# Inverse roots of three recurrent heads by small GpSimd operations, and two latent value products placed behind a head's turn

## The reference

```python
h_ml = mlstm_chunkwise(q_ml, k_ml, v_ml, gates[..., :ML_HEADS], gates[..., ML_HEADS:])
h_ml = rmsnorm(h_ml, ml_head_norm.reshape(ML_HEADS, ML_V))     # h * rsqrt(mean(h * h) + EPS), 4 heads of 128
h_ml = h_ml * jax.nn.sigmoid(o_ml)
...
h_mla = causal_block_attention(q, k, kv[..., MLA_NOPE:])       # 8 latent heads, 4 query blocks of 128
return jnp.concatenate([h_ml, h_mla], axis=-1) @ w_out
```

## Time and profile before

| | |
|---|---|
| median of 3 runs | 1511.03 us (1510.55 to 1511.44) |
| the profiled execution | 1513.8 us, of which the span is 1512.0 us |
| granted TensorE clock, mean | 0.998 |
| busy in the span | PE 99%, DVE 75%, ACT 50%, POOL 41% |
| chain that ended last | PE 87%, ACT 4%, DVE 4% |

### The profile page before, as it was taken

How to read it: one execution, slowest core, us unless ns; L and a number is a source line. 1 busy time by engine, 2 the same in 40 slices (tenths; PEclk the granted TensorE clock), 3 DMA queues, 4 the chain that set the end, 5 groups by cost and what they waited for, 6 DMA issues and landing times.

```text
span 1512.0 us, 20174 instructions
## 1 busy us (share of the span) xinstructions
PE 1491.3 (99%) x6978; PEld 1231.2 (81%) x6978; DVE 1128.0 (75%) x1872; ACT 751.4 (50%) x1255; POOL 626.8 (41%) x280
## 2 busy tenths in 40 slices
PE   9999999999999999999999999999999999999998
PEld 7888888878888887888888888787778888888887
DVE  5689999997865445776776768788755887777776
ACT  6554333455562345754544345464963745444434
POOL 3455444332334432144444445451534344444451
PEclk9999999999999999999999999999999999999999
DMA  5343233345443323333333123233643432333551
GB/s 212 98 124 99 95 94 95 92 157 157 157 157 98 98 83 112 104 93 97 112 98 109 52 85 97 84 98 93 186 140 105 142 117 90 109 122 114 142 136 56
DMA packets 77026, 170.40 MB, mean 113 GB/s; under 512 B 22660, under 2 KB 39172, under 8 KB 76680
## 3 DMA queue, kind: packets, MB, share of 16 engines
q1 hardware_dynamic: 75920, 165.64, 35.2%
q10 hardware_dynamic: 1016, 3.61, 0.7%
HBM read 154.54 MB, written 14.69 MB: 112 GB/s over the span
## 4 chain that ended last, share of the span: by engine, by line
PE 87%; ACT 4%; DVE 4%; issue 3%; POOL 1%; DMA 1%; SPq 0%; DVEq 0%; ACTq 0%; POOLq 0%
PE bank L795 86%; DMA w_raw<-in_stream 1%; POOL w_lo L655 1%; ACT w_hi L1604 1%; DVE x_sq L2359 0%; ACT l_probs L2129 0%; DVE bias L2441 0%; ACT l_probs L2135 0%; ACT dn_first L1898 0%; POOL res L764 0%; DMA dn_raw<-in_stream 0%; PE bank L1214 0%; DVE res_tok L3421 0%; PE bank L905 0%; ACT ml_square L2080 0%
## 5 line engine op out<-in xcount | busy, mean ns | idle before, releaser
L655 POOL TENSOR_TENSOR w_lo<-w_raw,w_hi 128x1024 fp32r<-128x1024 f32 x191 | 473.2, 2487 | 518.1 <-ACT w_hi L1604 510.4
L795 PE MATMUL bank<-a_hi,w_hi 128*128 128x512 f32 (+1 forms) x1120 | 444.8, 397 | 2.2 <-DVE a_lo L3284 1.8
L795 PE MATMUL bank<-a_hi,w_lo 128*128 128x512 f32 (+1 forms) x1120 | 431.4, 385 | 0.0
L795 PE MATMUL bank<-a_lo,w_hi 128*128 128x512 f32 (+1 forms) x1120 | 431.2, 385 | 0.0
L1604 ACT CAST w_hi<-w_raw 128x1024 fp32r<-128x1024 f32 x199 | 204.6, 1046 | 174.9 <-DMA w_raw<-in_stream 174.5
L795 PEld LDWEIGHTS bank<-a_hi,w_hi 128*128 128x128 f32 x1120 | 210.5, 188 | 49.0 <-issue 4.2
L795 PEld LDWEIGHTS bank<-a_lo,w_hi 128*128 128x128 f32 x1120 | 210.6, 188 | 45.2 <-issue 3.4
L795 PEld LDWEIGHTS bank<-a_hi,w_lo 128*128 128x128 f32 x1120 | 210.4, 188 | 42.6
L667 POOL TENSOR_TENSOR dn_rest<-dn_raw,dn_second 128x1024 fp32r<-128x1024 f32 x39 | 93.7, 2431 | 248.3 <-DVE dn_rest L2734 248.3
L795 PE MATMUL bank<-dn_rest,f_hi 128*128 128x512 f32 x364 | 141.7, 389 | 0.0
L1898 ACT CAST dn_first<-dn_raw 128x1024 fp32r<-128x1024 f32 x54 | 55.6, 1047 | 157.9 <-DVE dn_raw L2715 157.9
(11 more groups left out here) (428 smaller groups left out, 2763.5 us busy)
## 6 DMA issues: line engine op xcount, KB each, us to landing
w_raw<-in_stream SPq DMA_DIRECT2D x199, 512.0 KB, 3.5
dn_raw<-in_stream SPq DMA_DIRECT2D x56, 512.0 KB, 3.6
p_parts<-d_parts SPq DMA_DIRECT2D x8, 640.0 KB, 3.9
d_turned<-p_parts SPq DMA_DIRECT2D x32, 160.0 KB, 3.3
l_turned<-p_parts SPq DMA_DIRECT2D x32, 160.0 KB, 3.1
p_parts<-l_parts SPq DMA_DIRECT2D x8, 384.0 KB, 3.3
res<-in_xT ACTq DMA_DIRECT2D x1, 2048.0 KB, 9.1
p_parts<-l_parts SPq DMA_DIRECT2D x8, 256.0 KB, 2.4
```

Of the source, the lines that this page charges most:

```text
L655: nc.gpsimd.tensor_tensor(w_lo[:, j, :], w_raw[:, j, :], w_hi[:, j, :].bitcast(F32), ALU.subtract).then_inc(w_lo_done, 1)
L795: return nc.tensor.matmul(o, l, r, start=start, stop=stop)
```

## The change

For heads 0 to 2 the root leaves ACT and the inverse leaves DVE. DVE adds one operation at `st` 8: it reads the bits of `mcol[:, 2]` as an integer, times -0.5 plus a constant, which is a first guess of the inverse root. POOL refines it by ten operations on 128x4 values (`inverse_root`), each waiting for the one before on `root_step`; the tenth posts `ml_inv`, which DVE's scaling at `st` 9 waits for. Head 3 keeps ACT's root. In POOL's list the three refinements stand behind `remainder(CH["OM"])`, behind the first eight residual products, and behind the second eight.

The value products of latent heads 1 and 5 move: head 1 from step 13 to 14, head 5 from 29 to 28, in both cases between the turn of a recurrent head and `ml_values`. The cast and low part of latent head 1 move one step later; those of head 5 stay.

```diff
+VALUES_AT = {9: 0, 14: 1, 17: 2, 21: 3, 25: 4, 28: 5}
+SPLIT_AT = {10: 0, 15: 1, 18: 2, 22: 3, 26: 4, 30: 5}
...
+            def stepped(ins):
+                ins.then_inc(sems["root_step"], 1)
+                root_steps[0] += 1
+                pool.wait_ge(sems["root_step"], root_steps[0])
+
+            def inverse_root(h):
+                part, slope, x, y = (mcol[:, i, :] for i in range(4))
+                pool.wait_ge(sems["ml_var"], h + 1)
+                stepped(nc.gpsimd.tensor_tensor(part, y, y, ALU.mult))
+                stepped(nc.gpsimd.tensor_tensor(part, part, x, ALU.mult))
+                stepped(nc.gpsimd.tensor_scalar(slope, part, 0.375, -1.25, ALU.mult, ALU.add))
+                stepped(nc.gpsimd.tensor_tensor(part, part, slope, ALU.mult))
+                stepped(nc.gpsimd.tensor_scalar(part, part, 1.0, 1.875, ALU.mult, ALU.add))
+                stepped(nc.gpsimd.tensor_tensor(y, y, part, ALU.mult))
+                stepped(nc.gpsimd.tensor_tensor(part, y, y, ALU.mult))
+                stepped(nc.gpsimd.tensor_tensor(part, part, x, ALU.mult))
+                stepped(nc.gpsimd.tensor_scalar(part, part, -0.5, 1.5, ALU.mult, ALU.add))
+                nc.gpsimd.tensor_tensor(y, y, part, ALU.mult).then_inc(sems["ml_inv"], 1)
...
             remainder(CH["OM"], CH["OM"] % RING)
+            inverse_root(0)
             behind_diagonals(2)
...
             for unit in (17, 18):
                 second_residual(unit, residual_steps[unit])
+            inverse_root(1)
             behind_diagonals(3)
...
             for unit in (23, 24, 25, 26):
                 second_residual(unit, residual_steps[unit])
+            inverse_root(2)
             behind_diagonals(4)
...
-                turned = n == ML_START + ML_EVERY + turned_at(1)
+                turned = n in [ML_START + ML_EVERY * h + turned_at(h) for h in range(ML_HEADS - 1)]
...
-                if n % 4 == 1 and n >= 9:
-                    latent_values(n // 4 - 2)
+                if n in VALUES_AT:
+                    latent_values(VALUES_AT[n])
...
                 if st == 7:
                     act.wait_ge(sems["ml_out"], 4 * (h + 1))
+                    if h >= 1:
+                        act.wait_ge(sems["ml_inv"], h)
...
-                if st == 8:
+                if st == 8 and h == ML_HEADS - 1:
                     act.wait_ge(sems["ml_var"], h + 1)
                     A.activation(mcol[:, 3, :], mcol[:, 2, :], ACT.Sqrt).then_inc(sems["ml_root"], 1)
...
+                    if h < ML_HEADS - 1:
+                        chained(m)
+                        m = V.tensor_scalar(mcol[:, 3, :].bitcast(I32), mcol[:, 2, :].bitcast(I32), -0.5, ROOT_SEED,
+                                            ALU.mult, ALU.add)
+                    m.then_inc(sems["ml_var"], 1)
...
                 if st == 9:
-                    dve.wait_ge(sems["ml_root"], h + 1)
-                    V.reciprocal(mcol[:, 3, :], mcol[:, 3, :]).then_inc(sems["ml_inv"], 1)
+                    if h == ML_HEADS - 1:
+                        dve.wait_ge(sems["ml_root"], 1)
+                        V.reciprocal(mcol[:, 3, :], mcol[:, 3, :]).then_inc(sems["ml_inv"], 1)
                     dve.wait_ge(sems["ml_inv"], h + 1)
```

More of the change, by code:

```diff
@@ L205 @@
 squares_added ssq_added ssqg_added start_hi start_ready start_scaled stat_ready stat_root tap_done
-topk_step uq_out vm_rows wi_copied wi_turned x2_done x2_gained apart_hi apart_lo dn_sum dn_done dn_evac b_sum b_cast b_ready z_done z_root y_written half_done half_rooted half_sums part_sq part_ssq qk_tanh post_tree post_sq first_w first_x p_stored p_landed
+topk_step uq_out vm_rows wi_copied wi_turned x2_done x2_gained apart_hi apart_lo dn_sum dn_done dn_evac b_sum b_cast b_ready z_done z_root y_written half_done half_rooted half_sums part_sq part_ssq qk_tanh post_tree post_sq first_w first_x p_stored p_landed root_step
 """
@@ L222 @@
 GATES_AT = 1
+ROOT_SEED = float(0x5F3759DF)
 LATE_CASTS = 17
+VALUES_AT = {9: 0, 14: 1, 17: 2, 21: 3, 25: 4, 28: 5}
+SPLIT_AT = {10: 0, 15: 1, 18: 2, 22: 3, 26: 4, 30: 5}
 def turned_at(h):
@@ L705, in _ @@
             pool.wait_ge(sems["qk_rows_zeroed"], 2)
+            root_steps = [0]
+            def stepped(ins):
[15 more added lines that the diff above has]
+                nc.gpsimd.tensor_tensor(y, y, part, ALU.mult).then_inc(sems["ml_inv"], 1)
             for c in range(CH["OA"], CH["OM"]):
@@ L2148, in _ @@
             for n in range(4 * MLA_HEADS):
-                if n % 4 == 2 and n >= 10:
-                    latent_hi(n // 4 - 2)
+                if n in SPLIT_AT:
+                    latent_hi(SPLIT_AT[n])
                 latent_scaled(n)
@@ L3109, in ml_score_step @@
                     dve.wait_ge(sems["ml_den"], h + 1)
-                    V.scalar_tensor_tensor(out=mcol[:, 2, :], in0=mcol[:, 2, :], scalar=1.0 / ML_V,
-                                           in1=mcol[:, 1, :], op0=ALU.mult, op1=ALU.add).then_inc(sems["ml_var"], 1)
+                    m = V.scalar_tensor_tensor(out=mcol[:, 2, :], in0=mcol[:, 2, :], scalar=1.0 / ML_V,
+                                               in1=mcol[:, 1, :], op0=ALU.mult, op1=ALU.add)
+                    if h < ML_HEADS - 1:
[3 more added lines that the diff above has]
+                    m.then_inc(sems["ml_var"], 1)
             def ml_step(h, st):
@@ L3226, in _ @@
                     latent_turn(n - 1)
-                if n % 4 == 2 and n >= 10:
-                    latent_lo(n // 4 - 2)
+                if n in SPLIT_AT:
+                    latent_lo(SPLIT_AT[n])
                 ml_rest(n)
```

## The result

The changed kernel took 1516.03 us (median of 8 runs, 1514.06 to 1517.71); the kernel before beside it 1511.39 us (8 runs, 1510.55 to 1513.67). The ratio is 1.0027 with a 95% interval of 1.0018 to 1.0036, 2.7 to 5.4 us: slower. The forecast was 1510.5 us, and its range ended at 1514.0.

The account below looks back on a forecast made before the run. PE, busy 99%, bounds it; only its waits and slow clock can be won. 0.2 + 1.3 - 1.5 + 0.3 + 0.2 (last a guess for freer ACT) = 0.5 us off the median: 1510.5 us, range 1507.0 to 1514.0.

Parts of the forecast that it names:

- ACT's roots out: Heads 0 to 2: two table loads fewer per head, 7.7 us off ACT, so ACT bounds no `sT` any more.
- POOL's ten steps: Each refinement chain on POOL takes 2.6 us, 2.7 with the wait for `ml_var`.
- The ISA row: Rival, chance 0.12: MODIFY_POOL_CONFIG, inside head 0's chain, costs up to 3.3 us: 1513 to 1516; forecast took nothing.
- Head 0: At head 0 nothing waits for POOL's chain; latent head 1's products cover PE's 0.23 us for `hml`: gain 0.2 us.
- Head 1: Chain ends in time for DVE's scaling at head 1, PE's 1.31 us wait for `sT` goes: gain 1.3 us.
- Head 2: Third chain queues behind POOL's `rstd` products, `sT` comes as late as before: PE's 1.5 us lead is lost.
- The port: POOL's small chain operations beside DVE's diagonals can be held up: 0.3 us or so, put into the range.
- Latent head 5 moved: After head 2: covers 0.78 us for `hml`, later bares 1.0 us; gain 0 to 0.3, 1.6 to 1.8 if clock holds.
- The base of the sum: The 0.5 us gain was taken off the median, 2.8 us below the profiled execution's 1513.8 us.
- the clock's 1.6 us: After head 2's waits the granted clock was 0.54 for 3.4 us, costing 1.6 us.
- the 5.2 us to win: PE's four waits at heads 0 to 2, 3.6 us, with the slow clock 5.2 us: 0.34% of the kernel.

Follow-up runs that it names:

- e9: e5 with latent head 5's products back at step 29: 1510.48 us, ratio .9985 to the kernel before.
- e3: Kernel before with only the new places of latent heads 1 and 5, no root moved: 1513.67 us, ratio 1.0009 to the kernel before.
- e4: Changed kernel with latent head 1's products alone back at step 13: 1514.65 us, ratio 1.0018 to the kernel before.
- e8: e4 with one refinement left out of each POOL root, 6 steps for 10: 1512.59 us, ratio .9997 to the kernel before.
- e5: e4 with POOL's eight residual products of units 23 to 26 moved behind the last `ml_lo`: 1511.93 us, ratio .9997 to the kernel before.
- e12: Changed kernel with only POOL's eight residual products of units 23 to 26 moved behind the last `ml_lo`: 1514.23 us, ratio 1.0011 to the kernel before.
- e6: e4 with the third head's root given back to ACT and DVE: 1513.29 us, ratio 1.0003 to the kernel before.
- e2: Changed kernel with latent heads 1 and 5 put back where they stood, POOL's roots kept: 1514.40 us, ratio 1.0012 to the kernel before.

## Why the prediction was wrong, by its own steps

- *ACT's roots out*: right. Six table loads are gone between 1035 and 1130 us (7 before, 1 left), and where POOL's roots are in time (e9) `sT` comes earlier at heads 1 and 2.
- *POOL's ten steps*, 2.6 us: nearly right. Most took 0.20 us and 0.28 from start to start, two steps of a chain 0.30 to 0.33, and the chain 2.95 us at heads 0 and 2. At head 1 three took 0.33 to 0.62 and the chain 3.4 (1082.95 to 1086.36).
- *The ISA row*: nothing, as taken. Step 3 of head 0 began 0.30 us after step 2, which excludes the rival's 3.3 us. The first call's 6 us, of the Trainium skill ("GPSIMD Engine Reference", section "2.1 Instruction dispatch"), don't show here either. That the measured 1516.03 is the time which the prediction worked out for that rival, about 1516, is chance.
- *Head 0*, gain 0.2: **this step failed first**, by 2.1 us. I gave latent head 1's products to the 0.23 us that they would cover and left out what they covered where they stood. From DVE's scaling to `sT` it is 1067.35 - 1064.38 = 3.0 us of DVE's own queue, and PE got to the next score 1.8 us sooner than that. e3 shows 1.4 us by the order alone, and the changed kernel has 0.5 more with GpSimd's chain. That nothing waits for the chain here was wrong too: DVE's scaling at 1064.38 had waited 0.61 us for POOL. With the products back ahead of the turn (e4) neither shows.
- *Head 1*, gain 1.3: right in kind, 0.8 in size. A wait of 0.46 for `sT` stayed, because the chain was 0.7 us longer than my 2.7; with four steps fewer (e8) it is gone.
- *Head 2*, 1.5 given back: the mechanism, POOL's queue, is as described, and e5 and e12 show it, together with the port below. Its size was off. With head 1's 1.3 and head 5's share the sum had about zero for heads 1 and 2; by the ruler they were 1.1 us slower at the same clock.
- *The port*, 0.3 us and only in the range: **this is the other term that failed**, it was 2.4 us on DVE. I had the row (0.47 us), but looked for the harm in POOL's chain and took the excess of one operation, though three such operations of DVE stand in a row. My own step on POOL's queue had already moved the products onto all three. Queue and port end within 0.1 us of each other (1104.50 and 1104.53), so to take away only one of them would have won little in the changed kernel; no run does that there. e6 and e8 have the port's part without the queue's.
- *Latent head 5 moved*, 0 to 0.3: the bare wait for the last `sT` was 0.79 where I had about 1.0, but a gain doesn't show. Between e2 and e4, which differ by it alone, no difference can be told. Where the clock holds I had 1.6 to 1.8 us over a kernel whose clock fell; e3 has 12.88 - 11.84 = 1.0, and against a kept clock a loss of 0.5.
- The base of the sum: I took the clock's 1.6 us from one profiled execution and applied the difference to the median of others, which by their times mostly kept it. So the 5.2 us to win were 3.6 in half of the runs, and a clock that falls more often was a way to lose that I hardly counted. It cost 0.8, or 1.4 by the runs that stand beside the changed kernel.

All numbers together: 0.2 + 1.3 - 1.5 + 0.3 + 0.2 = 0.5 won was forecast; -1.9 + 0.8 - 1.9 - 0.8 = 3.8 lost was found.

What stays open: what decides whether the clock falls. Windows of the changed kernel (us, PE, PEld, DVE, ACT and POOL busy, PEclk, DMA share, GB/s):

```profile
1100.00:1110.00 10.00, 7.49 (x42) 5.51 (x40) 8.61 (x28) 6.21 (x20) 9.15 (x16) 1.00 0.42 120
...
1110.00:1115.00 5.00, 4.62 (x23) 4.30 (x24) 3.05 (x9) 4.08 (x11) 1.11 (x1) 0.66 0.57 185
```

PE was busy for 7.49 of 10 us and then had 0.66, mostly the lower level of 1.2 GHz. e4's profile has 7.10 of the same 10 us and kept 1.00 throughout, at 2.4 GHz; counted back from the start of head 2 as the changed kernel's 10 us are (1098.48 to 1108.48), it has 7.49 too. Runs of one program fall on both sides; only their share moves with the holes (11 of 11 in e2, 1 of 11 in e9).

## What to carry to other kernels

Before a filler is moved into one wait, compute what PE will wait for at the place that it leaves; here the cover there was worth eight times the wait that it was moved to (21.32 - 19.46 = 1.9 us against 0.23). A small chain given to an idle engine is cheap only if nothing long stands ahead of it in that engine's queue, and if that engine's long operations don't meet the short ones of the engine that feeds it: put the long ones behind. And profile the base more than once before a cost that only some runs have, such as a clock that falls in half of them, is counted as a prize.

## What the runs showed of the hardware that I had not expected

- A DVE operation of 128x4, 0.16 us, takes 1.20 us beside POOL's 128x512 products, ending with the product that runs; an int32 `tensor_scalar` with one tensor input did so as well (1.21 us).
- Dependent operations of 128x4 follow each other every 0.28 us on POOL and every 0.19 or 0.20 on DVE.
- The same program kept PE's clock in some runs and lost it in others, 1.9 us apart (two profiles of the kernel before: 1.00 throughout, and 0.54 over 3.4 us beside head 2, with PE busy for 1.37 of 3.4 us ahead of it in both).
- The time from the start to the stage varied by 2.3 us between profiles of kernels that don't differ there, most of it in the first 100 us (PE busy for 95.8 to 97.8 of them).
